# DeltaNet layer: the short convolution read from the projection's PSUM bank, its middle tap on ScalarE and three taps on VectorE

## The chip, the cores and the metric

The kernel runs on one core of a Trainium2 chip, in one launch. The metric is the device time of a run in microseconds. The engines are TensorE (PE), VectorE (DVE), ScalarE (ACT), GpSimd (POOL) and SyncE (SP), each with its own program, tied together by semaphores. SBUF is the working memory, PSUM holds eight banks of 128 x 512 fp32 that TensorE writes.

## What is computed

A two-layer encoder over 512 tokens of width 1024, in fp32. Layer 0 mixes tokens by windowed attention, layer 1 by a bidirectional gated DeltaNet; each ends with a mixture of 32 experts. The change touches only the head of the DeltaNet:

```
def short_conv(u, w):
    """Depthwise centred short convolution over the sequence; u (B,S,C), w (K,C)."""
    K, C = w.shape
    return lax.conv_general_dilated(u, w[:, None, :].astype(u.dtype), window_strides=(1,),
                                    padding=[(K // 2, K - 1 - K // 2)], ...)
...
    qkv, z, a, b = jnp.split(proj, [3 * D, 4 * D, 4 * D + 2 * H], axis=-1)
    qkv = jax.nn.silu(short_conv(qkv, conv_w))
    q, k, v = jnp.split(qkv, 3, axis=-1)
...
    q, k, v = l2norm(heads(q)), l2norm(heads(k)), heads(v)
```

With K = 4 an output token t is the sum of w0 u[t-2], w1 u[t-1], w2 u[t] and w3 u[t+1], with zeros outside the sequence, one set of weights per channel. The l2norm multiplies by (sum of squares + 1e-6) to the power -1/2; q is then also scaled by 128 to the power -1/2.

## The kernel before

The order of the work is written out by hand: each engine has a function (`gdn_pe`, `gdn_act`, `gdn_dve`, `gdn_pool`) whose instructions run in the order of the code, and every dependence is a semaphore `g[...]`. No scheduler moves anything.

The DeltaNet runs in two halves of four heads. A half begins with twelve **units** (`UNITS`): the four heads' q, then their k, then their v. A unit `U` (0 to 11 in the first half, 12 to 23 in the second) is one head's 128 channels by 512 tokens. `V` numbers the units of q and k, 16 in all, and is None for v. Behind the twelve units a half goes on with the chunk products, the inversion (`inverse_*`) and the scan (`scan_*`). After both halves come the gate z, the output projection and the second expert layer.

One unit goes through the engines so:

- TensorE: 24 products of 128 x 512 (lines 146 to 148, eight rows of weights in three split parts) into `bank[U % 4]`. Then it turns the SiLU result of unit U-1 to tokens (`to_tokens_pe`, line 1298, semaphore `silu`), and the normed tokens of unit U-2 back to channels (`to_channels_pe`, line 1313, semaphore `tok`; q and k only).
- ScalarE: in units 1 and 2 of each four it first rounds a part of the next weight panel (`split_high`, line 164). It copies the bank into the padded buffer `u_pad` (line 1432, semaphore `u`), squares the tokens of unit U-1 (line 1488), copies the channels of U-2 out of PSUM (line 1495), then waits for the convolution (`conv`) and applies SiLU (line 1440).
- VectorE: multiplies `u_pad` by tap 0 into `conv_acc` (line 1713), adds taps 1 to 3 (line 1716, each waits for the one before), sums the squares of unit U-1 (line 1765), adds the epsilon (line 1767, semaphore `ss`), waits for GpSimd (`rs`) and scales the tokens (line 1772).
- GpSimd: in units 1 and 2 of each four two subtractions for the next weight panel (`split_low`, line 170), and in each unit of q or k the power -1/2 (line 1556).

A product into a bank waits until ScalarE has copied the unit that was there four units before (`pe.wait_ge(g["u"], U - 3)`). During units 0 to 3 of the first half the gates' small computations go between (`gates_*`, `log_decays_dve`), and after unit 9 and 10 the decays (`decays_*`). The first exponents of the inversion (`exps_act`, line 1502) stand on ScalarE behind SiLU of the last unit.

Of the kernel before, what the change touches and what calls it, by code (L numbers as in the profile page):

```python
# [12 lines left out]
P = 128  # L13
# [31 lines left out]
def build(nc, ap, out):  # L45
    ctx = ExitStack()
    with ctx:
# [1063 lines left out]
        def k_decayed(hf, d):  # L1111
# [1 line left out]

        conv_l = Layout()
        conv_l.at = at0
        u_pad = conv_l.take(2, SEQ + CONV)
        conv_acc = conv_l.take(2, SEQ)
        silu_out = conv_l.take(2, SEQ)
        sq = conv_l.take(SEQ)
# [4 lines left out]
        gl.at = MASKS_AT + MASKS * P  # L1124
        small = {n: gl.take(TT, DIRS * B_HEADS) for n in
                 ("a", "e", "bias", "g", "gc", "tot", "eg", "lb", "dl", "kd")}
        qk_ss = gl.take(3, HALVES * 2 * HH, TT)
        o_ss = gl.take(3, TT, B_HEADS)
        conv_w = gl.take(CONV * CHANNELS)
        g_rows = sb("g_rows", [P, 2 * DIRS * B_HEADS + B_DK])  # L1130
# [2 lines left out]
        NB = DIRS * B_HEADS  # L1133

        g = {n: sem("gdn_" + n) for n in (
            "consts", "split", "small", "act", "dve", "pads",
# [67 lines left out]
        def gdn_pe(pe):  # L1204
# [6 lines left out]
            for hf in range(HALVES):  # L1211
                for U, _, w, h, V in UNITS[12 * hf:12 * hf + 12]:
                    n = GB + U // 4
                    if U >= 4:
                        pe.wait_ge(g["u"], U - 3)
                    if h == 0 and w == 0 and hf:
                        pe.wait_ge(g["s"], 6)
                        pe.wait_ge(g["qc"], 6)
                        pe.wait_ge(g["o2"], 8)
                    for c in range(KC):  # L1220
                        if h == 0:
                            split_done(pe, n, c)
                        last = three(pe, bank[U % 4][:, :], panel_parts(n, c, slice(h * P, (h + 1) * P)),
                                     ht_parts(3, c, slice(0, SEQ)), c == 0, c == KC - 1)
                    last.then_inc(g["proj"], 1)
                    if U % 12 >= 1:
                        to_tokens_pe(pe, UNITS[U - 1])
                    if U % 12 >= 2:
                        to_channels_pe(pe, UNITS[U - 2])
                    if U == 0:  # L1230
                        gates_pe(pe)
                    if U == 1:
                        gate_rows_pe(pe)
                    if U == 9:
                        decays_pe(pe)
                pe.wait_ge(g["kt"], 8 * (hf + 1))
                pe.wait_ge(g["dve"], 4)
                rows_pe(pe, 4 * hf, (6, 7))
                pe.wait_ge(g["u"], 12 * hf + 12)
                prods_pe(pe, 4 * hf, (0, 2))  # L1240
                to_tokens_pe(pe, UNITS[12 * hf + 11])
                pe.wait_ge(g["tok"], 12 * hf + 12)
                rows_pe(pe, 4 * hf + 1, (1, 4))
                prods_pe(pe, 4 * hf + 1, (3, 5))
                pe.wait_ge(g["exps"], 8 * hf + 2)
                rows_pe(pe, 4 * hf + 2, (6, 7))
# [176 lines left out]
        def gdn_act(act):  # L1423
            for hf in range(HALVES):
                for unit in UNITS[12 * hf:12 * hf + 12]:
                    U = unit[0]
                    split_high(act, GB + U // 4 + 1, QUARTERS[U % 4])
                    act.wait_ge(g["proj"], U + 1)
                    act.wait_ge(g["pads"], 1 + hf)
                    if U >= 2:  # L1430
                        act.wait_ge(g["conv"], U - 1)
                    act.copy(u_pad[:, U % 2, 2:2 + SEQ], bank[U % 4][:, :]).then_inc(g["u"], 1)
                    if U % 12 >= 1:
                        square_act(act, UNITS[U - 1])
                    if U % 12 >= 2:
# [39 lines left out]
        def decays_act(act):  # L1475
# [2 lines left out]
            act.activation(flat(small["dl"]), flat(small["tot"]), ACT.Exp)  # L1478
            act.activation(flat(small["kd"]), flat(small["kd"]), ACT.Exp).then_inc(g["act"], 1)

        def square_act(act, unit):
            U, hf, w, h, V = unit
            if V is None:
                return
            act.wait_ge(g["ta"], U + 1)
            if V >= 1:
                act.wait_ge(g["ss"], V)
            act.activation(sq, bank[4 + U % 2][:, :], ACT.Square).then_inc(g["sq"], 1)

        def channels_act(act, unit):  # L1490
            U, hf, w, h, V = unit
            if V is None:
                return
            act.wait_ge(g["tc"], V + 1)
            act.copy((k_tr if w else q_tr)[:, h, :], bank[6 + U % 2][:, :]).then_inc(g["kt"], 1)

        def exps_act(act, n, banks):
            hf, c = n // 4, chunk_of(n)
# [51 lines left out]
        def gdn_pool(pool, o):  # L1550
            for hf in range(HALVES):
                for U, _, w, h, V in UNITS[12 * hf:12 * hf + 12]:
                    split_low(pool, GB + U // 4 + 1, QUARTERS[U % 4])
                    if V is not None:
                        pool.wait_ge(g["ss"], V + 1)
                        pool.tensor_tensor(qk_ss[:, 2, V, :], qk_ss[:, 1, V, :], mhalf[:, 0:TT], ALU.pow
                                           ).then_inc(g["rs"], 1)
                if hf == 0:
                    pool.wait_ge(g["dve"], 3)
# [134 lines left out]

        def gdn_dve(dve, o):
            dve.wait_ge(g["small"], 1)
            dve.tensor_copy(conv_w, bank[5][:, 0:CONV * CHANNELS])
            for hf in range(HALVES):
                if hf:
                    dve.wait_ge(g["av"], 8)  # L1700
                for i in range(2):
                    dve.memset(u_pad[:, i, 0:2], 0.0)
                    last = dve.memset(u_pad[:, i, 2 + SEQ:CONV + SEQ], 0.0)
                last.then_inc(g["pads"], 1)
                for unit in UNITS[12 * hf:12 * hf + 12]:
                    U, _, w, h, V = unit
                    m = w * B_HEADS + hf * HH + h
                    dve.wait_ge(g["u"], U + 1)
                    dve.wait_ge(g["pads"], 1 + hf)
                    if U >= 2:  # L1710
                        dve.wait_ge(g["silu"], U - 1)
                    acc = conv_acc[:, U % 2, :]
                    o.step(dve.tensor_scalar(acc, u_pad[:, U % 2, 0:SEQ], conv_w[:, m:m + 1], None, ALU.mult))
                    for k in range(1, CONV):
                        at = k * CHANNELS + m
                        last = dve.scalar_tensor_tensor(out=acc, in0=u_pad[:, U % 2, k:k + SEQ],  # L1716
                                                        scalar=conv_w[:, at:at + 1], in1=acc,
                                                        op0=ALU.mult, op1=ALU.add)
                        if k < CONV - 1:
                            o.step(last)  # L1720
                    last.then_inc(g["conv"], 1)
                    if U % 12 >= 1:
# [34 lines left out]
        def tokens_dve(dve, o, unit):  # L1757
            U, hf, w, h, V = unit
            src = bank[4 + U % 2][:, :].rearrange("p (t n) -> p t n", t=TT)
            if V is None:  # L1760
# [4 lines left out]
            o.step(dve.tensor_reduce(qk_ss[:, 0, V, :], sq.rearrange("p (t n) -> p t n", t=TT), AX, ALU.add))  # L1765
            scale = 1.0 if w else float(B_DK)
            dve.tensor_scalar(qk_ss[:, 1, V, :], qk_ss[:, 0, V, :], EPS, scale, ALU.add, ALU.mult
                              ).then_inc(g["ss"], 1)
# [3 lines left out]
            dve.tensor_tensor(k_tok[:, h] if w else q_tok[:, U % 2], src,  # L1772
                              qk_ss[:, 2, V, :].unsqueeze(2).to_broadcast([P, TT, P]), ALU.mult
                              ).then_inc(g["tok"], 1)

        def sum_e(dve, n):
# [373 lines left out]
```

## Time and profile before

| what | value |
|---|---|
| median of 3 runs | 1538.74 us (1535.88 to 1540.78) |
| profiled execution, span from first to last instruction | 1541.2 us |
| busy share of the span: PE, DVE, ACT, POOL | 81%, 41%, 25%, 33% |
| instructions | 19154 |
| mean granted clock of TensorE | 0.911 |
| the twelve units, first and second half | about 630 to 735 us, 861 to 958 us |

The profiled execution's time stands here as its span; it is 2.5 us above the median of the runs. A busy share is an average over all stages. The two expert layers, where the memory traffic is near 400 GB/s, take the larger part of the span; the stage of the change is some 200 us of it.

### The profile page before, as it was taken

What the parts mean: (1) busy time and instruction counts of PE and PEld (TensorE: products, weight loads), DVE (VectorE), ACT (ScalarE), POOL (GpSimd) and SP (SyncE); (2) the same over time, 40 slices, a digit from 0 to 9 for tenths busy, and PEclk for the clock granted to TensorE, in tenths of its full rate; (3) what the DMA queues carried; (4) which work ended last, traced back from release to release, by engine and by line L of the source; (5) the groups of instructions that cost most, each with busy time, mean ns of one, the idle gap of its engine ahead of it and who ended that gap; (6) DMA issues with size and microseconds to landing.
All of it is one profiled execution on the core that took longest, in us unless ns stands there. A gap on an engine that the chain in (4) does not pass through costs nothing. (4 is left out here: it accounts for less than half of the span.)

```text
span 1541.2 us, 19154 instructions
## 1 busy us (share of the span) xinstructions
PE 1245.0 (81%) x7501; PEld 919.6 (60%) x7501; DVE 625.7 (41%) x1202; ACT 381.3 (25%) x796; POOL 508.5 (33%) x472
## 2 busy tenths in 40 slices
PE   5999989459887784798789988889979458888883
PEld 4776677435544452576688866678868434545451
DVE  4447642401111114477775576775282201111113
ACT  3325531011010012253433334332331011010010
POOL 1321000422222211045886355985440432222210
PEclk8999999579999997799999999999989579999997
DMA  6201001549999997011000130000321559999995
GB/s 207 77 34 55 1 21 60 214 167 382 396 398 387 394 411 303 0 55 55 1 1 1 55 109 2 1 1 1 110 69 55 218 190 386 404 398 392 388 408 218
DMA packets 66219, 270.65 MB, mean 176 GB/s; under 512 B 17133, under 2 KB 17389, under 8 KB 41553
## 3 DMA queue, kind: packets, MB, share of 16 engines
q1 hardware_dynamic: 52048, 246.25, 41.4%
q0 software_dynamic: 12064, 21.32, 4.1%
q10 hardware_dynamic: 2016, 1.84, 0.4%
q8 instruction: 62, 1.02, 0.3%
q14 instruction: 29, 0.23, 0.0%
HBM read 262.78 MB, written 23.35 MB: 186 GB/s over the span
## 5 line engine op out<-in xcount | busy, mean ns | idle before, releaser
L875 PE MATMUL bank<-ring,arena 128*64 128x256 f32 x2048 | 261.1, 408 | 73.6 <-issue 73.1
L875 PEld LDWEIGHTS bank<-ring,arena 128*64 128x64 f32 x2048 | 168.0, 141 | 147.7 <-issue 88.3
L760 POOL DMA_INDIRECT y_rows<-arena,idx_i x64 | 64.1, 1002 | 406.0 <-DVE arena L1025 391.2
L1318 PE MATMUL bank<-arena 128*128 128x128 f32 x1088 | 141.5, 287 | 14.9 <-DVE arena L1824 7.5
L1029 DVE TENSOR_TENSOR arena<-arena,bank 128x128 f32<-128x128 f32 x64 | 18.4, 287 | 326.8 <-ACT arena L952 321.6
L1318 PEld LDWEIGHTS bank<-arena 128*128 128x128 f32 x1088 | 132.9, 199 | 27.3 <-DVE arena L1824 11.6
L884 PE MATMUL bank<-ring,arena 128*64 128x512 f32 x512 | 123.9, 604 | 1.5 <-DVE arena L1034 1.5
L952 ACT ACTIVATE arena<-bank 128x128 f32<-128x128 f32 x64 | 17.7, 277 | 424.0 <-PE bank L875 381.3
L148 PE MATMUL bank<-ring_r,ht_r 128*128 128x512 f32 x288 | 113.5, 394 | 0.0
L1025 DVE COPY arena<-bank 128x512 f32<-128x512 f32 x64 | 44.3, 692 | 144.5 <-PE bank L884 144.5
L146 PE MATMUL bank<-ring_r,arena_r 128*128 128x512 f32 (+1 forms) x228 | 91.8, 403 | 3.4 <-DVE ring_r L170 3.4
L251 PE MATMUL bank<-ident,hn 128*128 128x128 f32 x192 | 38.5, 370 | 64.4 <-DVE hn L241 49.8
L147 PE MATMUL bank<-ring_r,arena_r 128*128 128x512 f32 x224 | 88.5, 395 | 0.0
L170 POOL TENSOR_TENSOR ring_r<-ring,ring_r 128x1024 fp32r<-128x1024 f32 x32 | 80.1, 2524 | 24.5 <-ACT ring_r L164 24.5
L867 PEld LDWEIGHTS bank<-ident,arena 64*128 64x128 f32 x512 | 61.3, 202 | 34.6 <-issue 25.1
L147 PE MATMUL bank<-ht_r,ring_r 128*128 128x512 f32 x192 | 77.9, 406 | 0.0
L867 PE MATMUL bank<-ident,arena 64*128 64x64 f32 x512 | 70.1, 278 | 9.3 <-DMA arena<-h_rows,idx_i 9.3
L251 PEld LDWEIGHTS bank<-ident,hn 128*128 128x128 f32 x192 | 33.0, 210 | 70.5 <-DVE hn L241 44.0
L1716 DVE SCALAR_TENSOR_TENSOR arena<-arena 128x512 f32<-128x512 f32 x72 | 72.8, 1011 | 2.6
L753 POOL DMA_INDIRECT arena<-h_rows,idx_i x64 | 60.7, 948 | 25.7 <-issue 18.9
L229 POOL TENSOR_TENSOR norm_s<-norm_s,mhalf 128x1 f32<-128x1 f32 x16 | 8.9, 555 | 178.1 <-DVE norm_s L238 178.1
L1629 POOL TENSOR_TENSOR arena<-ring,arena 128x512 f32<-128x512 f32 x48 | 61.9, 1310 | 6.9 <-PE bank L1318 6.9
(284 smaller groups left out, 2215.8 us busy)
## 6 DMA issues: line engine op xcount, KB each, us to landing
ring<-in_moe_w_gate SPq DMA_DIRECT2D x64, 1024.0 KB
ring<-in_moe_w_up SPq DMA_DIRECT2D x64, 1024.0 KB
ring<-in_moe_w_down SPq DMA_DIRECT2D x64, 1024.0 KB
ring<-in_gdn_w_in SPq DMA_DIRECT2D x8, 2048.0 KB
arena<-y_rows SPq DMA_DIRECT2D x16, 512.0 KB, 7.3
ring<-in_attn_w_in SPq DMA_DIRECT2D x3, 2048.0 KB
ring<-in_attn_w_out SPq DMA_DIRECT2D x2, 2048.0 KB
h_rows<-hn POOLq DMA_DIRECT2D x8, 512.0 KB, 13.9
```

Source lines behind the costliest of these rows:

```text
L146: pe.matmul(dst, a[0], b[0], start=start, stop=False)
L147: pe.matmul(dst, a[0], b[1], start=False, stop=False)
L148: return pe.matmul(dst, a[1], b[0], start=False, stop=stop)
L170: eng.tensor_tensor(panel(n, False, True)[:, c, :], panel(n)[:, c, :], panel(n, True, True)[:, c, :].bitcast(F32), ALU.subtract).then_inc( ...
L251: last = pe.transpose(b[:, j * P:(j + 1) * P], hn[:, t, half * 4 + j::KC], ident[:, :])
L760: pool.indirect_dma_start(out=y_rows[l], out_offset=bass.IndirectOffsetOnAxis(ap=idx_i[:, 1, e:e + 1], axis=0), in_=y_out[:, e % RING, :], ...
L867: last = pe.transpose(bank[0][:, c * SLOTS:(c + 1) * SLOTS], xg[0:SLOTS, i, c::KC], ident[0:SLOTS, 0:SLOTS])
L875: last = pe.matmul(bank[1][m * SLOTS:(m + 1) * SLOTS, 0:2 * P].rearrange("p (w n) -> p w n", w=2), xgt[:, i, c * SLOTS:(c + 1) * SLOTS], w ...
L884: last = pe.matmul(bank[3][half * SLOTS:(half + 1) * SLOTS, :], hidden_t[:, i, m * SLOTS:(m + 1) * SLOTS], d[:, m, half * HALF:(half + 1) ...
L1318: last = pe.matmul(bank[b][:, h * P:(h + 1) * P], lhs(h), rhs(h), start=True, stop=True)
L1629: pool.tensor_tensor(lm[slot], lt_of(n), by_head(level[l]), ALU.mult).then_inc(g["lm"], 1)
L1716: last = dve.scalar_tensor_tensor(out=acc, in0=u_pad[:, U % 2, k:k + SEQ], scalar=conv_w[:, at:at + 1], in1=acc, op0=ALU.mult, op1=ALU.add)
```

## The change

The padded copy `u_pad` is gone. ScalarE's evacuation of the bank writes tap 2 times the bank into `conv_acc`. VectorE then adds taps 1, 0 and 3 in this order, each read from the bank itself over the tokens for which it is inside the sequence (511, 510 and 511). The bank is given back to TensorE when VectorE is done (`conv`), not when ScalarE is (`u`); the first key products of a half wait for `conv` too. The epsilon is added on GpSimd ahead of the power, and the factor 128 to the power -1/2 of q is put into ScalarE's copy of the channels. In the second half the wait for the scan's last reads (`av`) moves from VectorE's memsets to ScalarE's first evacuation.

```diff
@@ gdn_pe
                     if U >= 4:
-                        pe.wait_ge(g["u"], U - 3)
+                        pe.wait_ge(g["conv"], U - 3)
...
-                pe.wait_ge(g["u"], 12 * hf + 12)
+                pe.wait_ge(g["conv"], 12 * hf + 12)
                 prods_pe(pe, 4 * hf, (0, 2))
@@ gdn_act
                     act.wait_ge(g["proj"], U + 1)
-                    act.wait_ge(g["pads"], 1 + hf)
+                    if U == 0:
+                        act.wait_ge(g["taps"], 1)
+                    if U == 12:
+                        act.wait_ge(g["av"], 8)
                     if U >= 2:
-                        act.wait_ge(g["conv"], U - 1)
-                    act.copy(u_pad[:, U % 2, 2:2 + SEQ], bank[U % 4][:, :]).then_inc(g["u"], 1)
+                        act.wait_ge(g["silu"], U - 1)
+                    act.activation(conv_acc[:, U % 2, :], bank[U % 4][:, :], ACT.Copy, scale=tap(2, unit)
+                                   ).then_inc(g["u"], 1)
...
+        def tap(k, unit):
+            U, hf, w, h, V = unit
+            at = k * CHANNELS + w * B_HEADS + hf * HH + h
+            return conv_w[:, at:at + 1]
@@ channels_act
-            act.copy((k_tr if w else q_tr)[:, h, :], bank[6 + U % 2][:, :]).then_inc(g["kt"], 1)
+            act.activation((k_tr if w else q_tr)[:, h, :], bank[6 + U % 2][:, :], ACT.Copy,
+                           scale=1.0 if w else B_DK ** -0.5).then_inc(g["kt"], 1)
@@ gdn_pool
                         pool.wait_ge(g["ss"], V + 1)
-                        pool.tensor_tensor(qk_ss[:, 2, V, :], qk_ss[:, 1, V, :], mhalf[:, 0:TT], ALU.pow
+                        o.step(pool.tensor_scalar(qk_ss[:, 1, V, :], qk_ss[:, 0, V, :], EPS, 0.0, ALU.add, ALU.add))
+                        pool.tensor_tensor(qk_ss[:, 1, V, :], qk_ss[:, 1, V, :], mhalf[:, 0:TT], ALU.pow
                                            ).then_inc(g["rs"], 1)
@@ gdn_dve
-                for i in range(2):
-                    dve.memset(u_pad[:, i, 0:2], 0.0)
-                    last = dve.memset(u_pad[:, i, 2 + SEQ:CONV + SEQ], 0.0)
-                last.then_inc(g["pads"], 1)
...
                     dve.wait_ge(g["u"], U + 1)
-                    dve.wait_ge(g["pads"], 1 + hf)
-                    if U >= 2:
-                        dve.wait_ge(g["silu"], U - 1)
-                    acc = conv_acc[:, U % 2, :]
-                    o.step(dve.tensor_scalar(acc, u_pad[:, U % 2, 0:SEQ], conv_w[:, m:m + 1], None, ALU.mult))
-                    for k in range(1, CONV):
-                        at = k * CHANNELS + m
-                        last = dve.scalar_tensor_tensor(out=acc, in0=u_pad[:, U % 2, k:k + SEQ],
-                                                        scalar=conv_w[:, at:at + 1], in1=acc,
+                    for k in (1, 0, 3):
+                        to, of = (slice(2 - k, SEQ), slice(0, SEQ - 2 + k)) if k < 2 else (slice(0, SEQ - 1), slice(1, SEQ))
+                        acc = conv_acc[:, U % 2, to]
+                        last = dve.scalar_tensor_tensor(out=acc, in0=bank[U % 4][:, of], scalar=tap(k, unit), in1=acc,
                                                         op0=ALU.mult, op1=ALU.add)
```

On VectorE, this is one unit of q or k in the row, with the semaphores each instruction waits for; before:

```order
L1713 TENSOR_SCALAR arena<-arena 128x512 [waits gdn_silu,gdn_pads,gdn_u]
L1716 SCALAR_TENSOR_TENSOR arena<-arena 128x512 [waits dve_chain] x3
L1765 TENSOR_REDUCE arena<-arena 128x4 [waits gdn_sq]
L1767 TENSOR_SCALAR arena<-arena 128x4 [waits dve_chain]
L1772 TENSOR_TENSOR arena<-bank,arena 128x512 [waits gdn_rs]
```

And the same unit in the changed kernel:

```order
L1716 SCALAR_TENSOR_TENSOR arena<-bank,arena 128x511 [waits gdn_u]
L1716 SCALAR_TENSOR_TENSOR arena<-bank,arena 128x510 [waits dve_chain]
L1716 SCALAR_TENSOR_TENSOR arena<-bank,arena 128x511 [waits dve_chain]
L1764 TENSOR_REDUCE arena<-arena 128x4 [waits gdn_sq]
L1769 TENSOR_TENSOR arena<-bank,arena 128x512 [waits gdn_rs]
```

The first tap and the epsilon are gone from VectorE, and the three taps left read one tensor from a PSUM bank. (`arena` is the large SBUF buffer in which all working tensors lie, the tap weights and `conv_acc` too.)

On GpSimd, this is the place of two units of q, one of them with subtractions; before:

```order
L1556 TENSOR_TENSOR arena<-arena,mhalf 128x4 [waits gdn_ss]
L170 TENSOR_TENSOR ring_r<-ring,ring_r 128x1024 [waits panel_high] x2
L1556 TENSOR_TENSOR arena<-arena,mhalf 128x4 [waits gdn_ss]
```

And in the changed kernel:

```order
L1565 TENSOR_SCALAR arena<-arena 128x4 [waits gdn_ss]
L1566 TENSOR_TENSOR arena<-arena,mhalf 128x4 [waits pool_chain]
L170 TENSOR_TENSOR ring_r<-ring,ring_r 128x1024 [waits panel_high] x2
L1565 TENSOR_SCALAR arena<-arena 128x4 [waits gdn_ss]
L1566 TENSOR_TENSOR arena<-arena,mhalf 128x4 [waits pool_chain]
```

The epsilon stands ahead of each power, and the power waits for it.

## Rows read from the trace of the kernel before

**Rows 1.** The page, busy time of each engine.
```profile
PE 1245.0 (81%) x7501; PEld 919.6 (60%) x7501; DVE 625.7 (41%) x1202; ACT 381.3 (25%) x796; POOL 508.5 (33%) x472
```
**Rows 2.** Timeline of TensorE: start, duration, instruction, idle before and its releaser.
```profile
674.23 0.66 PE L1313 MATMUL bank<-ident,arena 128*128 128x128 f32 x4 [1.05 <-DVE arena L1772]
...
680.64 0.60 PE L1313 MATMUL bank<-ident,arena 128*128 128x128 f32 x4
...
686.99 0.60 PE L1313 MATMUL bank<-ident,arena 128*128 128x128 f32 x4
...
704.31 0.65 PE L1313 MATMUL bank<-ident,arena 128*128 128x128 f32 x4 [1.30 <-DVE arena L1772]
...
879.31 0.66 PE L1313 MATMUL bank<-ident,arena 128*128 128x128 f32 x4 [0.32 <-DVE arena L1772]
...
897.11 0.66 PE L1313 MATMUL bank<-ident,arena 128*128 128x128 f32 x4 [1.30 <-DVE arena L1772]
...
936.72 0.60 PE L1313 MATMUL bank<-ident,arena 128*128 128x128 f32 x4
...
951.52 0.66 PE L1298 MATMUL bank<-ident,arena 128*128 128x128 f32 x4 [2.83 <-ACT arena L1440]
```
**Rows 3.** Waits of the second half: total us, times, longest us.
```profile
ACT arena L1440 <- DVE arena L1716: 41.2, 12, 7.1
...
PE bank L1313 <- DVE arena L1772: 5.5, 5, 1.3
```
**Rows 4.** Timeline of VectorE, two units of the second half.
```profile
888.08 1.99 DVE L1713 TENSOR_SCALAR arena<-arena 128x512 f32<-128x512 f32 x1
890.10 4.34 DVE L1716 SCALAR_TENSOR_TENSOR arena<-arena 128x512 f32<-128x512 f32 x3
...
896.97 0.47 DVE L1713 TENSOR_SCALAR arena<-arena 128x512 f32<-128x512 f32 x1
897.48 2.33 DVE L1716 SCALAR_TENSOR_TENSOR arena<-arena 128x512 f32<-128x512 f32 x3
899.72 0.68 DVE L1765 TENSOR_REDUCE arena<-arena 128x4 f32<-128x512 f32 x1
900.44 0.17 DVE L1767 TENSOR_SCALAR arena<-arena 128x4 f32<-128x4 f32 x1
901.73 0.69 DVE L1772 TENSOR_TENSOR arena<-bank,arena 128x512 f32<-128x512 f32 x1 [1.12 <-POOL arena L1556]
```
**Rows 5.** Timeline of GpSimd in the same units.
```profile
887.40 4.91 POOL L170 TENSOR_TENSOR ring_r<-ring,ring_r 128x1024 fp32r<-128x1024 f32 x2
895.32 1.01 POOL L1556 TENSOR_TENSOR arena<-arena,mhalf 128x4 f32<-128x4 f32 x1 [3.00 <-DVE arena L1767]
```
**Rows 6.** Windows: length, PE, PEld, DVE, ACT, POOL busy, granted clock, DMA.
```profile
674.00:693.00 19.00, 18.77 (x92) 15.47 (x92) 14.87 (x25) 8.90 (x14) 6.89 (x4) 1.00 0.00 0
...
897.00:901.00 4.00, 3.89 (x13) 3.17 (x14) 3.47 (x7) 1.74 (x3) 0.32 (x1) 0.61 0.00 0
```
**Rows 7.** Single lines: count, minimum/median/maximum ns, first and last start.
```profile
L1716 DVE SCALAR_TENSOR_TENSOR arena<-arena x72: 750/752/2771, 639.6 to 954.6; 128x512 f32<-128x512 f32 x72
...
L1841 DVE SCALAR_TENSOR_TENSOR arena<-bank,stay,arena x40: 740/743/752, 755.8 to 1044.9; 128x512 f32<-128x512 f32 x40
...
L1432 ACT COPY arena<-bank x24: 565/586/589, 638.4 to 951.4; 128x512 f32<-128x512 f32 x24
...
L1519 ACT ACTIVATE arena<-arena,stay x40: 721/722/772, 746.2 to 1039.4; 128x512 f32<-128x512 f32 x40
```
**Rows 8.** Timelines of VectorE and GpSimd in the inversion.
```profile
978.22 0.74 DVE L1841 SCALAR_TENSOR_TENSOR arena<-bank,stay,arena 128x512 f32<-128x512 f32 x1
...
976.18 3.11 POOL L1604 TENSOR_SCALAR arena<-arena,move 128x512 f32<-128x512 f32 x2
```
**Rows 9.** Small GpSimd instructions, grouped: busy us, mean ns, idle before.
```profile
L596 POOL TENSOR_SCALAR arena<-arena 128x384 f32<-128x384 f32 x16 | 11.4, 716 | 54.5 <-DVE arena L541 53.9
...
L724 POOL IOTA arena<- 128x4 f32 x4 | 0.7, 173 | 0.0
```

More of the change, by code:

```diff
@@ L1115, in build @@
         conv_l.at = at0
-        u_pad = conv_l.take(2, SEQ + CONV)
         conv_acc = conv_l.take(2, SEQ)
@@ L1126, in build @@
                  ("a", "e", "bias", "g", "gc", "tot", "eg", "lb", "dl", "kd")}
-        qk_ss = gl.take(3, HALVES * 2 * HH, TT)
+        qk_ss = gl.take(2, HALVES * 2 * HH, TT)
         o_ss = gl.take(3, TT, B_HEADS)
@@ L1135, in build @@
         g = {n: sem("gdn_" + n) for n in (
-            "consts", "split", "small", "act", "dve", "pads",
+            "consts", "split", "small", "act", "dve", "taps",
             "proj", "u", "conv", "silu", "ta", "sq", "ss", "rs", "tok", "tc", "kt",
@@ L1696, in gdn_dve @@
             dve.wait_ge(g["small"], 1)
-            dve.tensor_copy(conv_w, bank[5][:, 0:CONV * CHANNELS])
+            dve.tensor_copy(conv_w, bank[5][:, 0:CONV * CHANNELS]).then_inc(g["taps"], 1)
+            dve.wait_ge(g["taps"], 1)
             for hf in range(HALVES):
-                if hf:
-                    dve.wait_ge(g["av"], 8)
-                for i in range(2):
-                    dve.memset(u_pad[:, i, 0:2], 0.0)
-                    last = dve.memset(u_pad[:, i, 2 + SEQ:CONV + SEQ], 0.0)
-                last.then_inc(g["pads"], 1)
                 for unit in UNITS[12 * hf:12 * hf + 12]:
-                    U, _, w, h, V = unit
-                    m = w * B_HEADS + hf * HH + h
+                    U = unit[0]
                     dve.wait_ge(g["u"], U + 1)
-                    dve.wait_ge(g["pads"], 1 + hf)
-                    if U >= 2:
-                        dve.wait_ge(g["silu"], U - 1)
-                    acc = conv_acc[:, U % 2, :]
-                    o.step(dve.tensor_scalar(acc, u_pad[:, U % 2, 0:SEQ], conv_w[:, m:m + 1], None, ALU.mult))
-                    for k in range(1, CONV):
-                        at = k * CHANNELS + m
-                        last = dve.scalar_tensor_tensor(out=acc, in0=u_pad[:, U % 2, k:k + SEQ],
-                                                        scalar=conv_w[:, at:at + 1], in1=acc,
+                    for k in (1, 0, 3):
+                        to, of = (slice(2 - k, SEQ), slice(0, SEQ - 2 + k)) if k < 2 else (slice(0, SEQ - 1), slice(1, SEQ))
+                        acc = conv_acc[:, U % 2, to]
+                        last = dve.scalar_tensor_tensor(out=acc, in0=bank[U % 4][:, of], scalar=tap(k, unit), in1=acc,
                                                         op0=ALU.mult, op1=ALU.add)
-                        if k < CONV - 1:
+                        if k < 3:
                             o.step(last)
@@ L1764, in tokens_dve @@
             dve.wait_ge(g["sq"], V + 1)
-            o.step(dve.tensor_reduce(qk_ss[:, 0, V, :], sq.rearrange("p (t n) -> p t n", t=TT), AX, ALU.add))
-            scale = 1.0 if w else float(B_DK)
-            dve.tensor_scalar(qk_ss[:, 1, V, :], qk_ss[:, 0, V, :], EPS, scale, ALU.add, ALU.mult
+            dve.tensor_reduce(qk_ss[:, 0, V, :], sq.rearrange("p (t n) -> p t n", t=TT), AX, ALU.add
                               ).then_inc(g["ss"], 1)
@@ L1772, in tokens_dve @@
             dve.tensor_tensor(k_tok[:, h] if w else q_tok[:, U % 2], src,
-                              qk_ss[:, 2, V, :].unsqueeze(2).to_broadcast([P, TT, P]), ALU.mult
+                              qk_ss[:, 1, V, :].unsqueeze(2).to_broadcast([P, TT, P]), ALU.mult
                               ).then_inc(g["tok"], 1)
```

## Prediction

> **What bounds the kernel now.** I read the page first. TensorE is busy for 81% of the span [rows 1], but that is a mean over stages, so the next view was the start of every 512-column product of the short-convolution stage. That stage runs twice: from 630 to 735 us for heads 0 to 3 and from 861 to 958 us for heads 4 to 7, twelve units each time. The turn of a unit back to channels (line 1313) comes once in each of the units that have one, so its starts are a ruler for the stage [rows 2]. Between 680.64 and 686.99 us TensorE runs without a gap, and one unit takes 6.35 us: its own work. But from 686.99 to 704.31 us two units take 17.32 us, and from 879.31 to 936.72 us seven intervals (eight such rows in all) take 57.41 us, 8.2 us each. In these units TensorE stands still, for SiLU on ScalarE and then for VectorE's scaled tokens: the latter 1.30 us at 897.11.
>
> The table of waits of the second half says who is at the root: ScalarE waited 41.2 us for VectorE's taps (line 1716), twelve times, and TensorE 5.5 us for VectorE's tokens [rows 3]. VectorE's own timeline shows why it is late [rows 4]. A free unit there is 0.47 us for the first tap, 2.33 for the three others, 0.68 for the sum of squares, 0.17 for the epsilon, a wait for GpSimd's power, 0.69 for the scaling: some 5.4 us, under TensorE's 6.35. But in the unit at 888.08 the first tap takes 1.99 and the three others 4.34 us, 3.5 us more than free. GpSimd's timeline has the cause [rows 5]: its two subtractions of the next weight panel (line 170) run from 887.40 to 892.31, and a tap that starts beside one ends about when the subtraction does. So a unit takes VectorE 8.9 us (888.08 to 896.97), TensorE stalls, and behind the stalls the granted clock of TensorE falls: 0.61 from 897 to 901 us, where the unbroken stretch 674 to 693 us had 1.00 [rows 6].
>
> Is it the subtraction, or any GpSimd work, that holds VectorE? The grouped rows tell [rows 7]: the 72 taps, with both tensor inputs in SBUF, have a median of 752 ns and a maximum of 2771. The 40 operations of line 1841 are of the same kind and size, with one input from a PSUM bank and one from SBUF, in a stage where GpSimd is nearly always busy: 740 to 752 ns, not one longer. At 978.22 such a one takes 0.74 us inside GpSimd's 3.11 us run that begins at 976.18 [rows 8].
>
> **The change part by part.** (1) The first tap leaves VectorE (24 instructions, 0.47 us free and 1.99 held in [rows 4]) and the other three read the PSUM bank. They become the form of line 1841, so I take 0.75 us each and no hold. With the hop between dependent ones that is 3 x 0.79 = 2.37 us in place of some 2.8 free and 6.3 held. The shift of a tap's input is not in line 1841; line 1716 has it from SBUF at 0.752, so I bound it by 0.74 and 0.75.
>
> The Trainium skill, "VectorE: DVE Perf Modes", section Rules for kernel authors, speaks against this: for many operations on a matmul's output it advises copying from PSUM to SBUF first. By it the three taps should cost more from PSUM. Here the fp32 two-input rows are 743 ns with a PSUM input and 752 without, so this trace doesn't bear it out for this form; only the single-input first tap was quicker from SBUF (0.47), and that one goes.
>
> (2) ScalarE's copy from the bank (586 ns) becomes a Copy with a column of scales. Line 1519 has such a scale, from SBUF, at 722 ns [rows 7]. I take 0.70, within 0.59 and 0.72. It adds some 0.1 us to the delay from product to SiLU. As load it is hidden: in the unbroken stretch ScalarE was busy for 8.90 of 19.00 us [rows 6].
>
> (3) The epsilon moves from VectorE (0.17 us) to GpSimd, as a 128x4 instruction with a wait behind it, ahead of the power. The trace has no such small tensor_scalar there. The nearest rows are the 128x4 iota at 0.17 us and the 128x384 tensor_scalar at 0.72 [rows 9]; the power, also 128x4, takes 1.01 [rows 5]. I take 0.25 plus 0.1 for the wait, nearer to the iota for its size, and keep 0.2 and 1.1 as bounds. It lies on a wait of VectorE, which keeps its next unit's taps queued: VectorE's unit is then 2.37 + 0.68 + 0.35 + 1.01 + 0.1 + 0.69 = 5.2 us, still under 6.35. GpSimd in a unit with subtractions has 4.91 + 0.35 + 1.01 + 0.1 = 6.4 us, a tie, in two units of four. Following units 12 to 16, TensorE's turn of unit 14 comes 0.5 us after its tokens are ready. With 1.1 us in place of 0.35 it would wait some 1 us, at three such pairs: 3 us in all.
>
> (4) The bank is free, and the first key products may start, only after the taps and not after the copy: 2.4 us later. The next product in a bank comes three units later, so cover is over 12 us. The key products behind unit 11 and unit 23 have no such cover: there I take 0.2 us in the second half, and up to 0.8 in the first.
>
> (5) The edge memsets go, while VectorE waits for the first product anyway: nothing.
>
> The sum, second half: seven intervals at 6.35 are 44.45 us in place of 57.41, and the first turn loses its 0.32 us wait: 13.3 us. Behind the last unit TensorE waited 2.83 us for SiLU of unit 22, whose taps were held [rows 2]; that wait goes, with about 0.5 us of shorter taps and the products of (4) against it: 3.4 less 0.2 or so, 3.3. Together 16.6 us.
> First half: 17.32 less 12.70 is 4.6 us; the wait of 1.05 us at 674.23 goes, with 0.6 before it, 1.7; the shorter taps of the last two units, 0.5 each, 1.0. Together 7.3 us. The gate computation on ScalarE around 663 us stays and keeps its stall.
> Sum: 24 us. Everything behind the stage is chained to it (the inversion, the next weights' loads), so it comes off whole. Against the profiled span of 1541.2 us that gives 1517.2; the runs' median is 2.5 us lower, so 1514.7.
>
> **The rivals.** *The taps from PSUM are held too*, since one input and the output are still in SBUF. Then GpSimd's round in such a unit is its subtractions, 4.91, the 3.00 us that it now idles before the power at 895.32 [rows 5] less one tap (0.79) and the epsilon (0.2), 0.35 for (3), and the power, 1.01: 8.3 us in place of 8.9. Six times 0.6 is 3.6 us, with 1 us at each half's end and 1 at the gates some 7 us: 1532. The 40 quiet rows of line 1841 speak against it. For it speaks only that those ran beside other GpSimd instructions than line 170. The Trainium skill, "SBUF — State Buffer", names two kinds of VectorE operation that exclude GpSimd, a 2-port mode and two SBUF inputs; the new taps would be neither.
>
> *The small GpSimd instruction is dear*: 1.1 us as in (3), 3 us of stalls and about 1 us in the tails: 1519. It is inside my range.
>
> *Slower*: with no stalls left TensorE runs some 70 us on end in each half, and its clock is taken down because of that. At the lower level a product of 24 instructions takes twice 5.45 us, so one unit costs 5.45 us. Four and a half of 24 units so would undo the gain, and 5.4 units (29 us) make it 0.3% slower, from there on it decides: 1544 with six. Against it: the clock was 1.00 in the unbroken 19 us from 674, and lower after gaps, not in dense work.
>
> *Nothing reaches the end*: the inversion behind the stage would have to start on something that the stage doesn't set, about 1538. Its first exponents wait for the last SiLU's engine and for GpSimd's spread, which waits for the last product; all move.
>
> **How the numbers follow.** Forecast, TensorE-bound units: 0.78 with the dear GpSimd instruction in it. Held taps 0.13; nothing 0.05; slower 0.04. A change under 0.3% (4.6 us) can't be told from none here; the three runs span as much. Held taps count half a tenth of their chance as same: faster 0.90, same 0.06, slower 0.04. The range: low end 1506, where two clock dips of the first half vanish as well (each about 1.5 us) with a luckier clock behind; high end 1527, with 1519 and then dips that stay, short of the held case's 1532. That leaves out about 0.2.
>
> **What would show it.** Line 1313 (its new number) every 6.35 us from the fifth unit on in both halves; taps of 0.74 to 0.76 us with a maximum under 0.8, also beside line 170; no wait of TensorE over 0.3 us for ScalarE or VectorE in the second half; the granted clock 1.00 there; the GpSimd epsilon under 0.4 us; ScalarE's evacuation at 0.7. The forecast is wrong if taps over 1 us remain, if the epsilon takes 1 us, or if the clock falls without a gap ahead of it.

## Result and the profile after

| | before | changed |
|---|---|---|
| median | 1537.31 us (1534.71 to 1540.78) | 1517.09 us (1516.02 to 1517.45) |
| ratio, 95% interval | | 0.9864 (0.9843 to 0.9886) |
| span of the profiled execution | 1541.2 us | 1515.2 us |
| granted clock, mean | 0.911 | 0.913 |

The change makes the kernel 20 us faster; forecast were 24 and a range of 1506 to 1527. A second comparison later gave 1516.06 against 1537.44 us, ratio 0.9864 (0.9849 to 0.9879). The two traces are 26.0 us apart in span. A span is some 1.6 us shorter than the device time of the same execution (1515.2 for 1516.79 us here), so a span isn't to be set against a median: in device time the traced execution of the changed kernel lies 0.3 us below its median, and that of the kernel before, by the same 1.6 us, an estimated 5.5 us above its median. The forecast isn't touched by this, since it is 24 us below the median that it started from. Differences within a stage are read from the traces below, the worth of the whole from the medians.

The timeline of TensorE in the second half of the changed kernel, in the columns of [rows 2] (line 1312 is what 1313 was, 1297 what 1298 was, 1317 what 1318 was, 1331 the row sums of the chunk products):

```profile
872.76 0.60 PE L1312 MATMUL bank<-ident,arena 128*128 128x128 f32 x4
...
879.12 0.60 PE L1312 MATMUL bank<-ident,arena 128*128 128x128 f32 x4
...
917.22 0.60 PE L1312 MATMUL bank<-ident,arena 128*128 128x128 f32 x4
...
929.04 0.60 PE L1297 MATMUL bank<-ident,arena 128*128 128x128 f32 x4
929.48 1.02 PE L1331 MATMUL bank<-arena 128*128 128x512 f32 x2
930.34 1.02 PE L1331 MATMUL bank<-arena,upper 128*128 128x512 f32 x2
932.33 0.38 PE L1317 MATMUL bank<-arena 128*128 128x128 f32 x1 [0.97 <-DVE arena L1716]
```

The seven intervals from 872.76 to 917.22 us take 44.46 us, 6.35 each; they were 57.41 [rows 2]. None of these eight rows has a wait in brackets. The wait of 2.83 us behind the last unit is gone too. New is the 0.97 us at 932.33: the key products wait for the last unit's taps, since by the changed semaphore the bank counts as read only then.

The windows of the changed kernel, columns as in [rows 6]:

```profile
855.00:930.00 75.00, 74.58 (x366) 62.25 (x367) 36.39 (x53) 35.65 (x52) 41.34 (x31) 1.00 0.24 85
```

TensorE was busy for 74.58 of 75 us, and the granted clock was 1.00 throughout, where [rows 6] have 0.61 behind the stalls.

Single lines of the changed kernel, in the columns of [rows 7]: the taps, ScalarE's evacuation with its scale, the epsilon and the power on GpSimd.

```profile
L1716 DVE SCALAR_TENSOR_TENSOR arena<-bank,arena x72: 735/749/752, 640.0 to 931.5; 128x511 f32<-128x511 f32 x48, 128x510 f32<-128x510 f32 x24
```
```profile
L1434 ACT ACTIVATE arena<-bank,arena x24: 668/688/690, 639.2 to 929.2; 128x512 f32<-128x512 f32 x24
```
```profile
L1565 POOL TENSOR_SCALAR arena<-arena x16: 236/236/252, 654.0 to 914.3; 128x4 f32<-128x4 f32 x16
```
```profile
L1566 POOL TENSOR_TENSOR arena<-arena,mhalf x16: 1030/1032/1047, 654.3 to 914.7; 128x4 f32<-128x4 f32 x16
```

The maximum of the taps is 752 ns, where it was 2771: not one of 72 is held. Counted one by one in the two traces: before, 12 of the 72 taps ran beside a GpSimd instruction that reads SBUF, 8 of them beside line 170 and 4 beside the multiplications that spread the decays (`spread_pool`, line 1584), and all 12 took 1.41 to 2.77 us; the other 60 took 0.75. In the changed kernel 35 taps ran beside such an instruction, 30 of them beside line 170, and none took over 0.752. Here is such a place, VectorE and then GpSimd:

```profile
877.95 0.69 DVE L1769 TENSOR_TENSOR arena<-bank,arena 128x512 f32<-128x512 f32 x1 [1.80 <-POOL arena L1566]
879.61 2.32 DVE L1716 SCALAR_TENSOR_TENSOR arena<-bank,arena 128x511 f32<-128x511 f32 x3 [0.96 <-ACT arena L1434]
881.84 0.68 DVE L1764 TENSOR_REDUCE arena<-arena 128x4 f32<-128x512 f32 x1
884.12 0.69 DVE L1769 TENSOR_TENSOR arena<-bank,arena 128x512 f32<-128x512 f32 x1 [1.60 <-POOL arena L1566]
```
```profile
877.89 4.76 POOL L170 TENSOR_TENSOR ring_r<-ring,ring_r 128x1024 fp32r<-128x1024 f32 x2
882.74 0.24 POOL L1565 TENSOR_SCALAR arena<-arena 128x4 f32<-128x4 f32 x1
883.06 1.03 POOL L1566 TENSOR_TENSOR arena<-arena,mhalf 128x4 f32<-128x4 f32 x1
```

The three taps take 2.32 us inside the subtractions' 4.76. VectorE now waits for ScalarE's evacuation (0.96), which waits for TensorE's products, so TensorE sets the pace here.

**Where the time went, by stage.** From the traces, between the turn of the tap weights (630.41 before, 631.08 after), the first exponent of the inversion (734.38, 725.95), the first product of the second half (861.47, 855.42) and the second half's first exponent (957.32, 934.26):

| stretch | before | changed | difference |
|---|---|---|---|
| units of the first half | 103.97 | 94.87 | 9.1 |
| inversion and scan | 127.09 | 129.47 | -2.4 |
| units of the second half | 95.85 | 78.84 | 17.0 |

The second half gives what was forecast (16.6), the first more than its 7.3. The inversion and scan between them, whose instructions are the same, give 2.4 us back. Some 0.8 of it comes within the inversion. At 780.38 us TensorE waits 1.53 us for VectorE (line 1821), where it waited 0.62 at the same place before (787.93 us, line 1824). Half of that looks like the hold of [rows 4] in another place: a VectorE instruction with two SBUF inputs (line 1787) starts at 778.60, just after a GpSimd instruction that reads SBUF (778.55), and takes 1.13 us; before, it started ahead of the GpSimd instruction (786.60 against 787.01) and took 0.68.

The rest is in the windows from 813 us on; here is the changed kernel:

```profile
813.00:822.00 9.00, 6.82 (x48) 5.88 (x48) 3.32 (x5) 2.83 (x5) 4.66 (x7) 0.91 0.00 0
822.00:830.00 8.00, 8.00 (x64) 7.86 (x64) 4.51 (x11) 0.69 (x2) 3.60 (x5) 0.89 0.01 3
```
```profile
820.50:823.70 3.20, 3.20 (x17) 3.20 (x17) 0.00 (x0) 1.06 (x2) 2.86 (x4) 0.50 0.00 0
```

The 0.9 of the two long windows is an average: from 820.50 to 823.70 us the granted clock is 0.50, the lower level, and from 813 to 820 and from 824 to 838 it is 1.00. It falls where the scan begins and TensorE works without a gap, behind a wait of 1.47 us for GpSimd at 819.88. The kernel before has the same wait at its scan's beginning (827.48 us), and a granted clock of 1.00 from 813 to 838 us. One of its lower spells lies in the inversion, where TensorE is busy for 3.68 of 8 us anyway (0.62 from 742.38 to 750.38 us), and the mean granted clock of the whole stretch is 0.96 in both. Which of the two a kernel gets isn't explained here: the inversion and scan took 127.1 to 127.3 us in the traces of before and of three kernels below, and 128.9 to 129.5, with such a spell in the scan, in those of the others.

### The profile page after: what moved, and what is told of

Its sections match the earlier page's. It is cut to its first block and busy times, and to the rows that moved or that the text cites. A ratio compares the mean times of both kernels' runs of the same rounds, so it can differ in the third digit from the quotient of the medians.

```text
span 1515.2 us, 19098 instructions
## 1 busy us (share of the span) xinstructions
PE 1244.6 (82%) x7501; PEld 920.6 (61%) x7501; DVE 581.3 (38%) x1154; ACT 384.2 (25%) x796; POOL 510.5 (34%) x488
## 5 line engine op out<-in xcount | busy, mean ns | idle before, releaser
L875 PE MATMUL bank<-ring,arena 128*64 128x256 f32 x2048 | 267.0, 415 | 68.4 <-issue 65.6
L1716 DVE SCALAR_TENSOR_TENSOR arena<-bank,arena 128x511 f32<-128x511 f32 (+1 forms) x72 | 53.9, 749 | 59.2 <-ACT arena L1434 57.5
```

The lines of the kernel that those rows point to most:

```text
L875: last = pe.matmul(bank[1][m * SLOTS:(m + 1) * SLOTS, 0:2 * P].rearrange("p (w n) -> p w n", w=2), xgt[:, i, c * SLOTS:(c + 1) * SLOTS], w ...
```

## Experiments

There are two theories. **The hold**: a VectorE instruction with two SBUF inputs is stopped while GpSimd runs its subtraction, one with a PSUM input isn't, and the gain is that. **The shorter program**: the gain is that VectorE has one instruction and half a microsecond less per unit. The first two kernels tell them apart from both sides. The ratios below are to the kernel before, run beside each.

**The middle tap alone, taps from SBUF.** The kernel before, with ScalarE writing both the padded copy and tap 2 times the bank:

```diff
-                    act.copy(u_pad[:, U % 2, 2:2 + SEQ], bank[U % 4][:, :]).then_inc(g["u"], 1)
...
+                    act.copy(u_pad[:, U % 2, 2:2 + SEQ], bank[U % 4][:, :])
...
+                    act.activation(conv_acc[:, U % 2, :], bank[U % 4][:, :], ACT.Copy,
+                                   scale=conv_w[:, at:at + 1]).then_inc(g["u"], 1)
...
-                    o.step(dve.tensor_scalar(acc, u_pad[:, U % 2, 0:SEQ], conv_w[:, m:m + 1], None, ALU.mult))
-                    for k in range(1, CONV):
+                    for k in (1, 0, 3):
```

> The kernel before with one part of the change: ScalarE writes the padded copy as before and then also tap 2 times the bank (one more instruction of about 0.69 us per unit); VectorE adds taps 1, 0 and 3 from the padded SBUF copy. Epsilon as before. Theory of the hold (a tap with two SBUF inputs is stopped while GpSimd subtracts, a tap with a PSUM input is not): the taps still show a maximum over 2 us beside line 170; such a unit takes 8.1 to 8.3 us instead of 8.9, TensorE still stalls, and the gain on the kernel before is 4 to 8 us. Rival theory (the gain is VectorE's shorter program: one instruction and 0.5 us less per unit, and the hold is a side show): nearly the whole gain of the change, 17 to 21 us, and TensorE near 6.35 us a unit.

Measured: 1532.18 us against 1538.52, ratio 0.9957 (0.994 to 0.9974): 6.3 us. VectorE has three taps as in the changed kernel (the epsilon still stands on it), and some 70% of the gain are missing. Its taps, and VectorE's and GpSimd's timelines in such a unit:

```profile
L1720 DVE SCALAR_TENSOR_TENSOR arena<-arena x72: 736/752/2775, 643.1 to 953.3; 128x512 f32<-128x512 f32 x72
```
```profile
891.95 5.83 DVE L1720 SCALAR_TENSOR_TENSOR arena<-arena 128x512 f32<-128x512 f32 x3
```
```profile
891.28 5.17 POOL L170 TENSOR_TENSOR ring_r<-ring,ring_r 128x1024 fp32r<-128x1024 f32 x2
```

Three taps take 5.83 us beside the subtractions, 3.5 more than free, and TensorE's turns there are 8.4 us apart (892.09 to 900.45 us). So with taps from SBUF the shorter program is worth 6 us, with ScalarE's second instruction of 0.69 us per unit against it, and the rest needs the PSUM input.

**No reading on GpSimd, all taps as before.** The kernel before with the subtractions of the six q, k, v panels replaced by constant fills of the same length:

```diff
...
+                if GB < n < GB + 7:
+                    low = panel(n, False, True)
+                    for part in (c, c):
+                        low_steps.append(0)
+                        eng.memset(low[:, part, :].bitcast(F32), 1e-4).then_inc(low_chain, 1)
+                        eng.wait_ge(low_chain, len(low_steps))
+                    eng.memset(low[:, 2 * q, :].bitcast(F32), 1e-4).then_inc(panel_low[LOW_BY[n]], 1)
+                    continue
                 eng.tensor_tensor(panel(n, False, True)[:, c, :], panel(n)[:, c, :],
```

> The kernel before, with GpSimd's subtractions for the six q, k, v panels (line 170) replaced by constant fills of the same length: two and a half fills of 0.98 us for each subtraction, each waiting for the one before, which read nothing. The low parts of the weights are a small constant instead of the rounding rest. VectorE's program is unchanged, all four taps from SBUF. Theory of the hold: without GpSimd reading SBUF beside them the three two-input taps stay at 0.75 us; the units come down to 6.35 to 6.6 us and 15 to 22 us of the change's gain appear with nothing of the change made (if the first tap, which has a single input and runs at twice the rate, is held by a fill too, each such unit loses up to 1.5 us and the gain is 10 to 15). Rival theory (shorter program): within 0.3% of the kernel before.

Measured: 1514.43 us, ratio 0.9843 (0.9818 to 0.9869): 24 us faster with nothing of the change in it. All its taps, then VectorE and GpSimd in one unit:

```profile
L1725 DVE SCALAR_TENSOR_TENSOR arena<-arena x72: 750/752/1411, 640.0 to 929.8; 128x512 f32<-128x512 f32 x72
```

```profile
869.67 1.04 DVE L1722 TENSOR_SCALAR arena<-arena 128x512 f32<-128x512 f32 x1 [0.43 <-ACT arena L1441]
870.75 2.33 DVE L1725 SCALAR_TENSOR_TENSOR arena<-arena 128x512 f32<-128x512 f32 x3
```
```profile
868.47 1.96 POOL L175 MEMSET ring_r<- 128x1024 f32 x2
870.49 0.69 POOL L177 MEMSET ring_r<- 128x512 f32 x1
871.12 1.96 POOL L175 MEMSET ring_r<- 128x1024 f32 x2
873.14 0.53 POOL L177 MEMSET ring_r<- 128x512 f32 x1
```

GpSimd is as long at work (868.47 to 873.67 us), and the three taps take 2.33 us beside the fills, as if alone. So did all 32 two-input taps that ran beside a fill: none took over 0.753 us. The three longer ones, 1.40 to 1.41 us, are those that ran beside the multiplications that spread the decays, which still read SBUF. The first tap, with a single SBUF input, is held until about the end of the fill: 1.04 us for 0.49. So a fill stops the single-input instruction and not the one with two inputs. This is at least the whole gain, by taking away GpSimd's reading alone. The shorter program as the cause of the gain, which said no change here, is out. The Trainium skill, "SBUF — State Buffer", section Who interferes with whom, states this pair: a 2-port mode contends with GpSimd in general, two SBUF inputs only with a GpSimd instruction that reads SBUF. These rows agree with both, if the first tap runs in such a mode, for which its 0.49 us against 0.75 from PSUM (next kernel) speaks.

**All four taps from PSUM on VectorE.** The changed kernel, ScalarE's evacuation left out and the middle tap done by VectorE:

```diff
-                    act.activation(conv_acc[:, U % 2, :], bank[U % 4][:, :], ACT.Copy, scale=tap(2, unit)
-                                   ).then_inc(g["u"], 1)
...
+                    o.step(dve.tensor_scalar(conv_acc[:, U % 2, :], bank[U % 4][:, :], tap(2, unit), None, ALU.mult))
```

> The changed kernel with the middle tap back on VectorE, read from the PSUM bank (tensor_scalar); ScalarE evacuates nothing. VectorE has all four taps, one more instruction than in the changed kernel, about 0.7 us (a single-input operation from PSUM, like line 1762's copy at 0.68). Theory of the hold: a unit of VectorE is 2.37 + 0.72 + 0.68 + 0.35 + 1.01 + 0.1 + 0.69 = 5.9 us, still under TensorE's 6.35, no tap is held, so the time stays within 0.3% of the changed kernel, 1514 to 1520 us. Rival theory (shorter program): it loses 0.5 us per unit or more, 12 us and up, towards 1530.

Measured: 1517.77 us, ratio 0.9859 (0.9835 to 0.9884), the changed kernel's time. The middle tap from PSUM takes 751 ns and VectorE has four taps again, as before; TensorE's turns stay 6.35 us apart in the second half. The tap on ScalarE, half of what the change does by its name, is worth nothing once the inputs come from PSUM.

**The epsilon back on VectorE.**

```diff
-                        o.step(pool.tensor_scalar(qk_ss[:, 1, V, :], qk_ss[:, 0, V, :], EPS, 0.0, ALU.add, ALU.add))
...
+            dve.tensor_scalar(qk_ss[:, 0, V, :], qk_ss[:, 0, V, :], EPS, 0.0, ALU.add, ALU.add
+                              ).then_inc(g["ss"], 1)
```

> The changed kernel with the epsilon back on VectorE (the factor of q stays on ScalarE). The extra GpSimd instruction goes, VectorE gets 0.17 us and a hop of 0.04 back in each of 16 units, and its wait for GpSimd falls from 1.47 to 1.12 us. TensorE is the bound in these units by the trace of the changed kernel, so all theories of a TensorE bound say no change: within 2 us of the changed kernel. If GpSimd's round (4.76 + 0.32 + 1.04 us, at most 6.2 of 6.35) were the real limit, it would be 1 to 3 us faster.

Measured: 1516.34 us, ratio 0.9849 (0.9825 to 0.9874): no change that can be told, as expected.

**The epsilon four times.** Three more small instructions, each adding zero, ahead of the power:

```diff
+                        for _ in range(3):
+                            o.step(pool.tensor_scalar(qk_ss[:, 1, V, :], qk_ss[:, 1, V, :], 0.0, 0.0, ALU.add, ALU.add))
```

> The changed kernel with GpSimd's small epsilon instruction four times in a row (the three others add zero), each waiting for the one before: 3 x 0.32 = 0.96 us more on GpSimd and in VectorE's wait, in each of 16 units. My step says that 1.1 us in place of 0.35 costs about 3 us; here it is 1.28. By it: GpSimd's round with subtractions is 4.76 + 1.28 + 1.04 = 7.1 us, over TensorE's 6.35, so in each pair of such units TensorE ends up waiting 0.5 to 1.2 us for the tokens, three or four pairs, 3 to 6 us over the changed kernel in all, units without subtractions stay at 6.35. If the slack that I worked out (0.5 us) is far too small, it is within 1 us of the changed kernel.

Measured: 1523.75 us, ratio 0.9909 (0.9886 to 0.9931), some 7 us over the changed kernel. TensorE there:

```profile
873.54 0.66 PE L1312 MATMUL bank<-ident,arena 128*128 128x128 f32 x4 [0.52 <-DVE arena L1771]
...
880.63 0.66 PE L1312 MATMUL bank<-ident,arena 128*128 128x128 f32 x4 [0.51 <-DVE arena L1771]
...
887.71 0.66 PE L1312 MATMUL bank<-ident,arena 128*128 128x128 f32 x4 [0.50 <-DVE arena L1771]
...
894.13 0.60 PE L1312 MATMUL bank<-ident,arena 128*128 128x128 f32 x4
```

The round with subtractions is 7.09 us (873.54 to 880.63), as worked out (7.1). But here three turns wait, not two: the one before the pair as well. In the second pair of this half two wait (907.76 and 914.84 us), and each turn of a pair comes 0.74 us later than 6.35 behind the one before, the first as much as the second. That is 3.9 us in the second half by the stage table's marks (82.75 us against 78.84) and 2.1 in the first, 6.0 in the units. So the changed kernel sits close to GpSimd's round (4.76 + 0.32 + 1.03 us of 6.35), and my price of stalls for a dear epsilon, 3 us, was half of what this one costs.

**Only the epsilon and q's factor moved, in the kernel before.**

```diff
...
+                        o.step(pool.tensor_scalar(qk_ss[:, 1, V, :], qk_ss[:, 0, V, :], EPS, 0.0, ALU.add, ALU.add))
                         pool.tensor_tensor(qk_ss[:, 2, V, :], qk_ss[:, 1, V, :], mhalf[:, 0:TT], ALU.pow
...
```

> The kernel before with only the epsilon moved to GpSimd and the factor of q to ScalarE's copy. Four taps from SBUF stay. A unit beside subtractions is bound by VectorE and GpSimd in turn: it loses 0.17 + 0.04 us of VectorE and gains 0.32 us of GpSimd and hop, so 0.1 us slower in some eight units: within 2 us of the kernel before. If this part had carried a share of the gain (a shorter VectorE program as the cause), it would be 3 us faster or more.

Measured: 1541.94 us, ratio 1.0031 (1.0018 to 1.0045). This missed the expectation, so it ran once more:

> The kernel before with the epsilon and q's factor moved, once more: its first run was 0.3% slower than the kernel before (interval 0.18% to 0.45%), while its profile has only some 1 us more in the stage. If the move itself costs 5 us the ratio stays at 1.003; if that was the choice of executions, it comes to 1.000 to 1.001.

Measured: 1541.53 us, ratio 1.0031 (1.002 to 1.0043). The loss of 4 to 5 us is real. Of the sign there is no doubt; of the place there is: the held units are 9.05 us apart, 0.15 more than before, and the trace has only 0.5 us more in the second half and none in the first. The one trace of the kernel before is of an execution above its median, which can hide a part. The remainder is open. This part of the change is a loss by itself, and beside PSUM taps it can't be told from none (the epsilon back on VectorE, above).

This kernel and the one with four taps from PSUM are also the closest pair for the main question. Both have four taps on VectorE, the epsilon on GpSimd and q's factor on ScalarE; they differ in where the taps read, and in ScalarE's padded copy that goes with it. From SBUF the ratio is 1.0031, from PSUM 0.9859: some 26 us between them.

**The key products earlier.** Their banks were last read by units 8 and 10 (20 and 22), so they need not wait for the last unit:

```diff
-                pe.wait_ge(g["conv"], 12 * hf + 12)
+                pe.wait_ge(g["conv"], 12 * hf + 11)
```

> The changed kernel with the key products behind the last unit of a half waiting for the taps of unit 10 (22) in place of unit 11 (23): their banks were last read by units 8 and 10. In the changed kernel TensorE waited 0.98 and 0.97 us there for VectorE. That wait goes; the last turn to tokens behind the products then waits for SiLU of the last unit, so 0.5 to 0.9 us earlier at the next rows, twice: 1 to 2 us faster than the changed kernel at the best, which the medians may not tell from none; the wait in the trace must be gone.

Measured: 1514.47 us, ratio 0.9844 (0.9821 to 0.9867). The waits of 0.98 and 0.97 us are gone from the trace. The median is 1.6 to 2.6 us lower than the changed kernel's two, but the intervals overlap, and the traces show no gain. TensorE three rows behind the key products of the second half, in the changed kernel and then in this one:

```profile
939.74 1.10 PE L1331 MATMUL bank<-ring,arena 128*128 128x512 f32 x2 [0.36 <-POOL ring L1594]
```
```profile
937.13 1.10 PE L1331 MATMUL bank<-ring,arena 128*128 128x512 f32 x2 [1.53 <-POOL ring L1594]
```

The turn of the last unit but one starts at 929.04 us in the one and at 926.44 in the other, so both rows come 10.7 us behind it: what TensorE no longer waits for VectorE, it waits for GpSimd.

**The gates from PSUM.** The hold should not be particular to taps. In the first half the gates' two instructions for absolute values have two SBUF inputs of 64 columns each and stand beside the subtractions. In the changed kernel:

```profile
656.37 1.41 DVE L1682 SCALAR_TENSOR_TENSOR arena<-arena 128x64 f32<-128x64 f32 x1
657.71 2.43 DVE L1684 SCALAR_TENSOR_TENSOR arena<-arena 128x64 f32<-128x64 f32 x1
```

The edit reads one input of each from the gates' bank:

```diff
+            o.step(dve.tensor_tensor(ab[:, :, 0:NB], ab[:, :, 0:NB], wide, ALU.add))
-            dve.scalar_tensor_tensor(out=sm["e"], in0=sm["a"], scalar=-1.0, in1=sm["a"], op0=ALU.mult,
+            dve.scalar_tensor_tensor(out=small["e"], in0=ab[:, :, 0:NB], scalar=-1.0, in1=small["a"], op0=ALU.mult,
...
-            dve.scalar_tensor_tensor(out=sm["bias"], in0=sm["lb"], scalar=-1.0, in1=sm["lb"], op0=ALU.mult,
+            dve.scalar_tensor_tensor(out=small["bias"], in0=ab[:, :, NB:], scalar=-1.0, in1=small["lb"], op0=ALU.mult,
```

> The changed kernel with the gates' two absolute values read from the PSUM bank of the gates (their sum with the bias is written back into that bank first, one more 128x64 instruction), so that neither has two SBUF inputs. In the changed kernel they stand beside line 170 and take 1.41 and 2.43 us for 64 columns; if the hold is a matter of two SBUF inputs they take about 0.2 us each now, the taps of unit 2 start 2.5 us earlier, and TensorE's waits of 1.43 and 0.57 us at the third and fourth turn to channels shrink to under 0.3: 1.5 to 2.3 us faster than the changed kernel. If any VectorE work on SBUF is stopped there, the rows stay long and nothing is gained.

> The changed kernel with the gates from PSUM and the key products waiting for the unit before the last (both edits above and earlier). 3 to 4 us faster than the changed kernel if the two add up: 1512 to 1514 us, the fastest so far.

> The changed kernel once more, unchanged, as the measure for the two below on the same chip. 1514 to 1519 us; ratio to the kernel before 0.984 to 0.989.

Measured side by side: changed kernel 1516.06 us, ratio 0.9864 (0.9849 to 0.9879); gates from PSUM 1511.98, ratio 0.9836 (0.9822 to 0.9849), the intervals just touch; with the key products earlier as well 1510.73, ratio 0.9822 (0.9808 to 0.9835), below the 1512 to 1514 expected. The rows of the gates' kernel, on the same subtraction:

```profile
656.19 0.23 DVE L1683 SCALAR_TENSOR_TENSOR arena<-bank,arena 128x64 f32<-128x64 f32 x1
656.33 0.21 DVE L1685 SCALAR_TENSOR_TENSOR arena<-bank,arena 128x64 f32<-128x64 f32 x1
```
```profile
654.87 4.75 POOL L170 TENSOR_TENSOR ring_r<-ring,ring_r 128x1024 fp32r<-128x1024 f32 x2
```

They take 0.23 and 0.21 us where they took 1.41 and 2.43. TensorE's waits of 1.44 and 0.57 us behind the gates are gone. The units of the first half take 92.61 us by the marks of the stage table, against 94.87 and 94.23 in the two traces of the changed kernel: 1.6 to 2.3 us, as expected. The medians have 4.1; the rest isn't placed, and part of it may be chance, since the intervals touch. The last kernel is the fastest of the study, 26.7 us under the kernel before.

## Why the prediction held, step by step

- **What bounds the kernel**: right. Free units at 6.35 us and held ones at 8.9 were most of the matter, and the clock behind the stalls came back with them.
- **(1) taps from PSUM**: right in mechanism and size: 0.749 us, three in 2.32 us, none held. It is the step that carries the gain, as the fills and the SBUF taps show.
- **The rule for copying first**: the row of the Trainium skill that the prediction cites ("VectorE: DVE Perf Modes", section Rules for kernel authors) gives the copy as one of two ways, beside accepting the rate from PSUM; the prediction named only the copy. Four taps from PSUM took the changed kernel's time, four from SBUF 20 us more, and 26 with the epsilon placed alike. For this form, beside a reading GpSimd, the measurement decides against the copy.
- **(2) the evacuation**: 0.688 us for my 0.70, hidden.
- **(3) the epsilon**: 0.236 us and a hop of 0.09 to the next instruction, for 0.25 and 0.1; hidden in the changed kernel. Its price if dear was set too low: I gave the first turn of a pair 0.5 us of slack, and in the kernel with four epsilons it was as late as the second.
- **(4) the bank's release**: 0.97 and 0.98 us of wait; I had 0.2 and up to 0.8. The sign "no wait over 0.3 us in the second half" failed with it. It cost nothing there: without it TensorE waits for GpSimd instead.
- **The sum**: the second half 17.0 us for 16.6, of which the seven intervals are 12.95 as forecast, what lies ahead of them 0.50 for 0.3 and what lies behind them 3.56 for 3.3. The first half 9.1 for 7.3: 4.62 between the turns at 686.99 and 704.31 us as forecast, 2.59 ahead of them for 1.7, and 1.89 behind for 1.0. Ahead of them a fall of the clock went that I had left in: the unit's 24 products from 665.43 us took 7.31 us before, and 5.72 from 665.59 after. The other fall of the first half stayed (granted clock 0.50 from 707.8 to 711 us).
- **"Everything behind the stage ... comes off whole"**: this is the step that failed. The inversion and scan behind the first half gave back 2.4 us, some 1.5 of it with the clock's lower spell in the scan, the rest with a longer wait for VectorE in the inversion. That the traces' sum, 23.7 us up to the second half's first exponent, is so near to 24 is luck: the units gave 2.2 us more than forecast and this took 2.4.
- **The rest**: the medians have 20 to 21 us. The last 3 us can't be placed, since only one execution of the kernel before is traced, and it is slower than its median.
- **The rivals**: held taps, out by 752 ns at the most. A clock lowered by unbroken work, out: 1.00 over 75 us. Nothing reaching the end, out.

## What to carry to other kernels

Before an instruction on VectorE is made shorter, look at its longest case beside its median: 752 and 2771 ns in one row said that the cost was not the work but who ran beside it. Where GpSimd reads SBUF at length, give VectorE's two-input instructions one input from PSUM; a matmul's result need not be copied out for it. When such a stage is freed, compute the next engine's round at once: here GpSimd's was at 96% of TensorE's, and 1 us more on it cost 7. And a wait that is gone from a trace is a gain only if no other has grown behind it.

## What the runs showed of the hardware that was not expected

- The hold goes by what each side touches: a GpSimd subtraction stops two-input taps and the single-input first tap from SBUF (1.99 us for 0.47 [rows 4]), a GpSimd fill only the single-input one (1.04 us for 0.49; 32 two-input taps at 0.75). The tap weights are read from SBUF too, as a column of scales, and don't count as a second SBUF input: none of 35 such taps was held.
- It costs GpSimd as well: two subtractions took 5.17 us beside three held SBUF taps, 4.91 beside the taps of before [rows 5], 4.76 beside taps from PSUM.
- A length of 64 columns is no protection: 0.2 us of work took 2.43 us.
- The order of the two starts seems to decide, by one pair of rows: a two-input instruction that began 0.41 us ahead of GpSimd's took 0.68 us, the same one 0.05 us behind it 1.13.
- The granted clock was 0.50 for 3.2 us and more at the beginning of the scan, where before it was 1.00, though the instructions there are the same.
